# The routing weights' buffer, begun 32 bytes later in each partition of SBUF

## What is computed

```
def retrieve_chunk(xc):
    ...
    expert = e1 * PEER_KEYS + e2
    g = jax.nn.softmax(top_s, axis=-1)
    u = jnp.take(expert_u, expert, axis=0)
    act = jax.nn.gelu(jnp.einsum('thkd,td->thk', u, xc).astype(jnp.float32), approximate=False)
    w = (g * act).astype(xc.dtype)
    return jnp.einsum('thk,thkd->td', w, jnp.take(expert_v, expert, axis=0))
```

## Time and profile before

| | us |
|---|---|
| median of three runs | 2519.1 |
| lowest, highest | 2513.16, 2525.83 |
| the profiled execution, its own time | 2511.46 |
| its span, first to last instruction | 2509.7 |
| TensorE (PE) busy | 2452.7 (98%) |
| weight loads (PEld) busy | 2275.2 (91%) |
| VectorE, ScalarE, GpSimd busy | 1801.3, 1245.6, 1230.9 |
| mean granted TensorE clock, share of full speed | 0.983 |

### The profile page before, as it was taken

One profiled execution on the slowest core, in us unless ns is written; L12 is line 12 of the kernel. 1 busy time (PEld: TensorE's weight loads), 2 busy tenths in 40 slices (PEclk: granted clock), 3 DMA queues, 4 the chain that ended last, 5 costly groups with the idle time before them and its releaser, 6 DMA issues.

```text
span 2509.7 us, 47109 instructions
## 1 busy us (share of the span) xinstructions
PE 2452.7 (98%) x18074; PEld 2275.2 (91%) x18074; DVE 1801.3 (72%) x3366; ACT 1245.6 (50%) x2150; POOL 1230.9 (49%) x525
## 2 busy tenths in 40 slices
PE   7999999989999999999999999999999999999999
PEld 7999999988999999998888888889999999888887
DVE  6858674578759699987676775563988999555555
ACT  5335543456555544445444454545454444454444
POOL 5537787645789977750000024456997776100000
PEclk9999999989999999999999998999999999999999
DMA  5325697732466654558777753335665455566664
GB/s 166 136 85 184 233 335 262 271 111 90 147 193 194 192 157 155 154 164 271 259 252 254 259 182 101 98 113 159 192 194 171 154 159 153 189 190 192 192 193 143
DMA packets 126063, 457.94 MB, mean 182 GB/s; under 512 B 13984, under 2 KB 15392, under 8 KB 125600
## 3 DMA queue, kind: packets, MB, share of 16 engines
q1 hardware_dynamic: 118512, 425.56, 53.1%
q10 hardware_dynamic: 7344, 29.49, 3.3%
HBM read 453.95 MB, written 1.05 MB: 181 GB/s over the span
## 4 chain that ended last, share of the span: by engine, by line
PE 89%; DVE 7%; ACT 2%; issue 1%; DMA 1%; POOL 0%; SPq 0%; DVEq 0%; ACTq 0%
PE mm L1298 28%; PE ms L1338 28%; PE mm L813 20%; PE ms L1319 3%; DVE work L1999 1%; DVE hs L1999 1%; PE ms L820 1%; PE ms L828 1%; DVE scratch L1999 1%; PE mm L820 1%; DVE work L1993 1%; PE mm L982 1%; PE mm L1276 1%; DVE work L1996 1%; PE mm L861 0%
## 5 line engine op out<-in xcount | busy, mean ns | idle before, releaser
L1942 POOL TENSOR_TENSOR low<-ring,high 128x1024 fp32r<-128x1024 f32 (+1 forms) x502 | 1217.5, 2437 | 908.6 <-ACT high L1549 748.3
L1807 ACT ACTIVATE high<-ring 128x1024 fp32r<-128x1024 f32 x506 | 535.8, 1059 | 353.7 <-PE ms L1338 321.2
L1298 PE MATMUL mm<-hs,high 128*128 128x256 f32 x4096 | 520.4, 280 | 0.7 <-ACT work L1558 0.7
L1338 PE MATMUL ms<-high,wts 128*128 128x512 f32 x2048 | 510.5, 391 | 0.0
L2584 DVE TENSOR_TENSOR low<-ring,high 128x1024 fp32r<-128x1024 f32 x256 | 313.3, 1225 | 247.4 <-ACT high L1807 247.2
L1298 PEld LDWEIGHTS mm<-hs,high 128*128 128x128 f32 x4096 | 486.7, 188 | 0.9 <-ACT work L1558 0.9
L1338 PEld LDWEIGHTS ms<-high,wts 128*128 128x128 f32 x2048 | 384.1, 188 | 84.0 <-DVE wts L2575 0.2
L1549 ACT ACTIVATE high<-ring 128x1024 fp32r<-128x1024 f32 (+1 forms) x252 | 258.6, 1030 | 125.1 <-PE mm L813 93.9
L813 PE MATMUL mm<-hs,high 128*128 128x256 f32 x2192 | 286.0, 284 | 3.0 <-DVE parts L1993 1.8
L1338 PE MATMUL ms<-low,wts 128*128 128x512 f32 x1024 | 276.3, 392 | 0.0
L813 PEld LDWEIGHTS mm<-hs,high 128*128 128x128 f32 x2192 | 268.1, 192 | 7.7 <-ACT high L1549 3.7
(11 more groups left out here) (342 smaller groups left out, 3040.4 us busy)
## 6 DMA issues: line engine op xcount, KB each, us to landing
ring<-w_peer_experts SPq DMA_DIRECT2D x512, 512.0 KB, 4.1
work<-w_mod ACTq DMA_DIRECT2D x48, 512.0 KB, 5.7
ring<-w_late_mods SPq DMA_DIRECT2D x48, 512.0 KB, 4.5
ring<-w_ffn_up SPq DMA_DIRECT2D x44, 512.0 KB, 5.0
ring<-w_peer_q SPq DMA_DIRECT2D x32, 512.0 KB, 3.6
ring<-w_fox_in SPq DMA_DIRECT2D x32, 512.0 KB, 3.5
ring<-w_lru_in SPq DMA_DIRECT2D x22, 512.0 KB, 3.5
ring<-w_gates SPq DMA_DIRECT2D x16, 512.0 KB, 3.5
```

The source lines that it names most:

```text
L1298: ins_ = pe.matmul(mm[:, s_ % BANKS, 0:T], w_[:, k * P:(k + 1) * P], hs[:, b_, k, :], start=pass_ == 0 and k == 0, stop=pass_ == 2 and k = ...
L1338: ins_ = pe.matmul(ms[:, 2 * c + half, :], wts[:, s_ % 3, b_, c * P:(c + 1) * P], v_[:, half * 512:(half + 1) * 512], start=s_ == 0 and pa ...
L1807: act.activation(high[:, (q0 + i) % CUT, :], ring[:, n_ % RAW, :], ACT.Copy) \
L1942: pool.tensor_tensor(low[0:rows, cut_slot, 0:width], ring[0:rows, raw_slot, 0:width], high[0:rows, cut_slot, 0:width].bitcast(F32), ALU.su ...
```

## The change

One buffer of 8 float32 (32 bytes) a partition is taken ahead of `wts`. Nothing reads or writes it. `wts` begins at byte 215904 in place of 215872, which is 96 in place of 64 against multiples of 128. `slots` and every buffer ahead of it stay where they are, `wts` is the last buffer in SBUF, and no instruction is added, removed or moved.

```diff
         hs = sb("hs", [P, 2, KD, T], F32R)
         with nc.sbuf_tensor("slots", [P, 6, T], F32) as slots:
             pass
+        sb("off_line", [P, 8])
         wts = sb("wts", [P, 3, 2, T], F32R)
```

## The result

The changed kernel takes 2530.1 us, the median of 17 runs (2521.4 to 2538.7), beside 2521.6 us for the kernel before in 17 runs. The ratio is 1.0041, with a 95% interval of 1.0025 to 1.0057: 6 to 14 us more. (The two medians by themselves are 8.5 us apart, 0.34%, which is inside the interval.) The profiled execution has a span of 2519.6 us, before it was 2509.7.

The account below looks back on a forecast made before the run. The prediction took TensorE's own pace in the value loops as the bound; its terms, 0 (writes) + 0 (load) + 0 (pair of reads), changed nothing, so it forecast 2517 us, range 2487 to 2536.

Parts of the forecast that it names:

- What bounds the kernel: Value loops of both layers: 3072 matmuls, 703.7 us, wholly on the chain of waits, bound by TensorE's own pace, 228.9 ns each.
- The writes of `wts` and the load: ScalarE and VectorE writes of 404 and 418 ns and the 188 ns weight load: covered by TensorE, term 0.
- Rival C: Writes of `wts` slow down and lose their cover, needing over 685 ns more a tile in layer 0; 1 in 100.
- rival D: The pad might push `wts` by 64 bytes, to 0, if buffers lie at multiples of 64; 1 in 100.
- The pair of reads: Value loop, moving columns streaming while `wts` loads: bounds -47.9 to +37 us, taken as 0.
- six starts: Value loop reaches one pace from five beginnings in layer 0 and one in layer 1, so probably from a shifted address too.
- the products of the earlier trace: Same product, same addresses modulo 512, ran at two paces: 66 matmuls in 7.77 or 7.49 us, 4.2 ns apart each.
- Rival B: Value loop's two reads fall into a slower step: 5 ns a matmul, +15 us, 2534 us; chance 0.21 together with Rival C.
- 258-column rows: Products with rows 1032 bytes apart take 120.2 ns; moving starts off 64 bytes seem to cost 1.7 to 6.1 ns.
- Rival A: Value loop's two reads fall into a quicker step: -7 to -48 us, middle -27 us, 2490 us; chance 0.27.
- the row of two quick products: Value loop's nearest pace below the present: two 256-column products for one of 512, 226.6 ns, -2.3 ns, -7.1 us.

## Why the prediction was wrong

**What bounds the kernel.** Right. The value loops lie on the chain whole, and nothing else had to move for the time to move: 4.4 ns x 3072 = 13.5 us there, and 2521.6 x 0.0041 = 10.3 us, 6.3 to 14.4 by the interval, in the time.

**The writes of `wts` and the load.** Right at 0: 418 and 400 ns, and 187 ns for the load, with idle time ahead of it before and after. Rival C has nothing to stand on, and rival D's doubt is settled: a pad of 64 bytes in place of 32 gives another pace (226.7 against 233.3 ns), so the change did shift `wts` by 32 bytes and not by 64.

**The pair of reads.** This is the step that failed: the prediction put the term at 0, and it measured 4.4 ns a matmul, +13.5 us. It said: "two streams' relative position is set by their starting times as much as by their addresses", and took the same pace from six starts as a sign that a shifted address would come to that pace too. The six starts had one thing in common, the distance of 192 bytes, and by the map that is what made their pace. A steady pace from many beginnings showed that the beginning does not matter in this loop; it said nothing of the address, which never varied. In the products of the earlier trace rows the beginning, or something else that is no address, does matter, and the hidden loop is of that kind. That two streams of matmuls can differ in this was there to be seen.

**Rival B.** It has the right place, size and sign: one step, priced at 4.2 ns and +12.9 us, measured at 4.4 ns and +13.5. Its reason was wrong. It said that a start off a multiple of 64 bytes costs more, from the 258-column rows. With everything 32 bytes later the pace is the old one although `wts` is off such a multiple, and at distance 64, where it is on one, it is slow. Those 258-column rows shift by 8 bytes each, so their distances vary too; whether that is what makes them slow was not tested. Rival A's mechanism exists as well, but at another place: distance 0, -2.2 ns a matmul, where the pace meets the row of two quick products (226.6 ns) that the prediction named.

**The Trainium skill.** The page "SBUF — State Buffer", section "Who interferes with whom", has matmul and weight load on independent ports. By it the distance could not matter; the runs have 226.7 to 234.3 ns for it, and the measurement decides.

**The size of the change.** The forecast of 2517 us, in effect no change, was made from a profiled execution and a median of three. The prediction called 0.5% what can be told; with 17 runs a change of 0.41% is clear of zero. The measured 2530.1 us does lie in the stated range of 2487 to 2536, but only because the range was stretched to take in rival B; that is no merit of the forecast. The rivals' sums also slip by 2 us: A's 2490 counts from 2517 and B's 2534 from 2519.

## What to carry to other kernels

The pace of back-to-back float32r matmuls can hang on the distance between the stationary and the moving operand's start, modulo 256 bytes: by 3% in this value loop (226.7 to 234.3 ns) and by 6% with 256 moving columns (113.3 to 120.0). The good distance was not the same for 256 and 512 moving columns. Where such a loop is on the chain whole, try a few paddings ahead of one operand and read the pace in a profile of each. Judge them by the loop's own piece in the chain rather than by the run's time, which spreads by 15 us and more. Layer 1's value loop repeats to 0.05 us at one distance (348.19 to 348.22 us at 0 in six profiles). But profile twice, because a loop can have two paces at one address, as the hidden loop has.

## What the runs showed that was not expected

- Many paces are multiples of 16 ticks of 2.4 GHz, or of a third of 16: 544, 549.3 and 560 ticks for 512 columns, 272, 282.7 and 288 (113.3, 117.8 and 120.0 ns) for 256. Distances 8, 96 and 128 do not fit (553.6, 562.3, 557.7), nor do the 118.3 and 118.7 ns of 256 columns at 32 and 128. The reason is open.
- The pattern is modulo 256 bytes: 192 and 448 agree to 0.01 us in 351.59, 64 and 192 do not.
- A much shorter weight load did not quicken the stream by more than 0.4 ns: 228.5 ns with 64 columns, 231.1 with 32, 228.9 with 128.
- One kernel's hidden loop ran at 117.8 ns in one execution and at 113.3 in another, from the first tile to the last before the placing begins.
